# Gated attention's fine levels packed by 32 tokens, eight places for the merge masks of the WKV scan, and two long reciprocals in four column parts

## The chip, the cores and the metric

The kernel runs on one core of a Trainium2 chip. The metric is device time in microseconds, the median of several executions; smaller is better. One further execution was taken with the hardware profiler, and every row below is from that one.

## The reference

Sequence of 512 tokens, width 1024, float32. A first block has two layers (three mixers side by side, then an MLP and a gated embedding), a second block has a banded attention, an RWKV-7 mixer (WKV) and two convolutional FFNs. What the change touches is, cut to its core:

```
# HGRN2 ("gated attention"), 4 heads of 64, in each of the two layers of the first block
G = cumsum(log_f); decay[l, s] = exp(G[l] - G[s]) for s <= l, else 0
A[l, s] = sum_d q[l, d] * decay[l, s, d] * k[s, d]
o = inter + A @ v;  h_out = head_rms_norm(o) * silu(gate)
# mLSTM ("memory"), 4 heads of 64: weighted scores, a denominator, head_rms_norm, a gate
# sliding window attention with a sink, 8 heads, window 128
# WKV, 16 heads of 64, forwards and backwards over the sequence, in the second block:
state = state * w + (state @ a) b^T + v k^T;  y = state @ r
```

## The kernel before

The program is a row of stages with a barrier of all engines between two. Nearly all stages are dense matrix products, which are not changed. Two kinds of stage are.

**The mixers' stage** (`mixers`, once in each of the two layers). Everything lies in SBUF; the tokens are four tiles of 128 (`NT`). Three programs are woven on each engine: attention (16 groups `n` of a head pair and a token tile), gated attention, and memory (8 units, a head pair by a key tile). Each program is a generator that yields a beat before each step, and `weave` emits the steps in the order of their beats; so the constants `MEMORY, UNIT = 0, 4`, `ATTEND, GROUP = 38, 3` and `SCORE, LEVEL = 1, 5.5` set the order on every engine. Engines run their lists in order and wait on semaphores.

Gated attention builds `A` by levels `n` = 0 to 9. Level 0 is the diagonal; level `n` from 1 to 7 has half-width `w = 2^(n-1)` and gives the pairs of a key in the left and a query in the right half of each block of `2w` tokens; levels 8 and 9 are the pairs of different tiles of 128. A level is: VectorE forms two halves of `diffs` (`differ`, L1200 and L1201), ScalarE takes `exp` (L1170), VectorE makes `q_dec` (`decayed`, L1208), TensorE multiplies (`scores`, L1258), and VectorE copies the masked entries from PSUM into `A` (`copy`, L1216). The fine levels 0 to 7 are done for whole 128x128 tiles in two halves `x` (two tiles each), and the second half's products wait until the first half has left PSUM. Levels 8 and 9 are moved by ScalarE (L1181). Then come the sum `A @ v` (L1277), the squares' sums (L1284), a root with an activation table of its own, a reciprocal of 128x512 (L1233), its spread over the heads (L1289) and the gate. Memory ends in the same way: root (L1344), reciprocal (L1379), spread (L1448). Attention's group is: scores (L1063, L1067), peaks (L1118), `exp` on ScalarE, shares (L1135), turn (L1079), take (L1034), outputs (L1094). GpSimd does nothing in this stage.

**The WKV stage** (`rwkv_heads`), a software pipeline over 8 head pairs. Its longest part merges inverses of 64x64 blocks in five levels: 20 units `u` per iteration, in the order of `merge_order`, each with `inner` (L2779) and `outer` (L2792) products on TensorE and two copies on ScalarE. `inner` reads a masked block `NM` that GpSimd makes (`part`, L3057), into one of `PARTS_AHEAD = 4` places. Between the parts GpSimd does other work of the next head pair in `scale_beat` (L3067, L3072, L3076, L3079), at fixed places of the same order; the first two of these (L3067) wait for VectorE.

Of the kernel before, what the change touches and what calls it, by code (L numbers as in the profile page):

```python
# [15 lines left out]
P = 128  # L16
# [49 lines left out]
HG_LEVELS = 7  # L66
# [3 lines left out]
MASKS, MASKS_W = columns(("causal", P), ("levels", HG_LEVELS * P), ("pick", 4 * P), ("groups", P), ("sums", 2 * P), ("back", 2 * P))  # L70
# [5 lines left out]
def constants():  # L76
# [31 lines left out]
    for level in range(HG_LEVELS):  # L108
        w = 1 << level
        same = i // (2 * w) == j // (2 * w)  # L110
        m[:, MASKS["levels"] + level * P:MASKS["levels"] + (level + 1) * P] = same & (i % (2 * w) < w) & (j % (2 * w) >= w)
# [284 lines left out]
SCORE, LEVEL = 1, 5.5  # L396
# [562 lines left out]
def mixers(nc, m, f, dst, table=None):  # L959
# [3 lines left out]
               "g_cleared", "g_diffs", "g_exp", "g_q_ready", "g_scored", "g_copied", "g_moved", "g_summed", "g_taken",  # L963
# [5 lines left out]
    with ExitStack() as tmp, stage(nc, f"mixers{f.layer}", *signals) as (block, s):  # L969
# [179 lines left out]
        A = sb("A", [P, 2, 2, 4, P])  # L1149
# [3 lines left out]
        halves_of = [[(0, 0), (1, 1)], [(2, 2), (3, 3)]]  # L1153
        pieces = [halves_of] * (1 + HG_LEVELS) + [[[(0, 1), (2, 3)]], [[(0, 2), (1, 2)], [(0, 3), (1, 3)]]]
        numbers = [(n, x) for n in range(len(widths)) for x in range(len(pieces[n]))]
        masked = 2 * (1 + HG_LEVELS)

# [8 lines left out]

        def gated_act(act):
# [4 lines left out]
            for n in range(len(widths)):  # L1172
                if n >= 1:
                    yield SCORE + LEVEL * n - 0.5
                    exps(n)
                if n > HG_LEVELS:
                    for x in range(len(pieces[n])):
                        yield SCORE + LEVEL * n + 2.4 + 1.4 * x
                        number = numbers.index((n, x))
                        act.wait_ge(s["g_scored"], number + 1)  # L1180
                        nc.scalar.activation(across[:, number - masked, :, :, :], scores_two(), ACT.Copy).then_inc(s["g_moved"], 1)  # L1181
# [8 lines left out]
        def gated_dve(dve):  # L1190
            yield 0
            nc.vector.memset(A[:], 0.0).then_inc(s["g_cleared"], 1)
            nc.vector.memset(q_dec[:], 0.0).then_inc(s["g_cleared"], 1)

            def differ(n):
                w = widths[n]
                if n >= 3:
                    dve.wait_ge(s["g_scored"], 2 * n - 2)
# [11 lines left out]
            def copy(n, x):  # L1210
                dve.wait_ge(s["g_scored"], 2 * n + x + 1)
                if n == 0:
                    dve.wait_ge(s["g_cleared"], 1)
                at = MASKS["levels"] + (n - 1) * P
                which = (m.masks[:, at:at + P] if n else m.ident).bitcast(I32).unsqueeze(1).unsqueeze(1).broadcast_to([P, 2, 4, P])
                nc.vector.copy_predicated(A[:, x, :, :, :], which, scores_two()).then_inc(s["g_copied"], 1)  # L1216

            for n in range(len(widths)):
# [3 lines left out]
                if n <= HG_LEVELS:  # L1222
                    yield SCORE + LEVEL * n + 2.4
                    copy(n, 0)
                if n + 1 < len(widths):
                    yield SCORE + LEVEL * n + 3
                    differ(n + 1)
                if n <= HG_LEVELS:
                    yield SCORE + LEVEL * n + 3.8
                    copy(n, 1)  # L1230
# [12 lines left out]
        def gated_pe(pe):  # L1243
            def scores(n, x):
                number = numbers.index((n, x))
                if 1 <= number <= masked:
                    pe.wait_ge(s["g_copied"], number)
                elif number:
                    pe.wait_ge(s["g_moved"], number - masked)
                if n >= 1:  # L1250
                    pe.wait_ge(s["g_q_ready"], n)
                kk, qq = (diffs[:, n % 2, :, :], q_dec[:, n % 2, :, :]) if n else (key, hq)
                for i, (source, to) in enumerate(pieces[n][x]):
# [13 lines left out]
            pe.wait_ge(s["g_copied"], masked)  # L1267
            places = {}
            for n, x in numbers:
                for i, pair in enumerate(pieces[n][x]):  # L1270
                    places[pair] = A[:, x, :, 2 * i:2 * i + 2, :] if n <= HG_LEVELS else across[:, numbers.index((n, x)) - masked, :, 2 * i:2 * i + 2, :]
# [15 lines left out]
            pe.wait_ge(s["g_rstd"], 1)  # L1287
# [58 lines left out]
        def memory_dve(dve):  # L1346
# [32 lines left out]
            nc.vector.reciprocal(den[:], den[:]).then_inc(s["c_rstd"], 1)  # L1379
# [9 lines left out]
        def memory_pe(pe):  # L1389
# [56 lines left out]
            pe.wait_ge(s["c_rstd"], 1)  # L1446
            for t in range(2):
                nc.tensor.matmul(m.ps[:, 6 + t, :], const("back", t * P), den[:], start=True, stop=True).then_inc(s["c_back"], 1)  # L1448

# [1061 lines left out]
PARTS_AHEAD = 4  # L2511
# [16 lines left out]
def rwkv_heads(nc, m, a, vec, keep, x_kept):  # L2528


    with ExitStack() as tmp:
# [66 lines left out]
        with stage(nc, "heads", "tables_in", "x_back", f"loaded*8", "set_up",  # L2598
# [445 lines left out]
            def _(pool):  # L3044
# [38 lines left out]
                for i in iterations:  # L3083
# [391 lines left out]
```

## Time and profile before

| what | value |
|---|---|
| median of 3 runs | 3319.1 us (3315.32 to 3321.97) |
| profiled execution, its own time | 3314.73 us |
| its span | 3312.9 us |
| TensorE busy | 3059.1 us, 92% of the span |
| VectorE, ScalarE, GpSimd busy | 1858.7, 1388.3, 630.9 us |
| mean granted clock of TensorE | 0.969 of full speed |

The span is that of the profile; the execution's own time is 1.8 us more than it. The mixers' stages lie at about 164 to 300 us and 924 to 1061 us, the WKV stage at about 2380 to 2870 us.

### The profile page before, as it was taken

How to read it: one execution, taken by the hardware profiler on the slowest of the kernel's cores; microseconds unless marked ns; L12 is line 12 of the kernel's file. 1: busy time of each engine (PE TensorE's matmuls, PEld its weight loads, DVE VectorE, ACT ScalarE, POOL GpSimd, SP SyncE). 2: the span in 40 equal slices, each digit the busy share in tenths (PEclk: the TensorE clock that was granted, in tenths of full speed). 3: DMA queues.
4: the chain of work that ended last, by engine and by line, in shares of the span. 5: the costliest groups of instructions: out<-in, count | busy, mean ns of one | idle time of the engine just before them, and what ended most of it. 6: DMA issues, size and time to landing. Idle time of an engine off the chain costs nothing. (4 is left out here: it accounts for less than half of the span.)

```text
span 3312.9 us, 57356 instructions
## 1 busy us (share of the span) xinstructions
PE 3059.1 (92%) x24238; PEld 2427.1 (73%) x24238; DVE 1858.7 (56%) x2689; ACT 1388.3 (42%) x2363; POOL 630.9 (19%) x528
## 2 busy tenths in 40 slices
PE   8979999999978999999989999979688888799999
PEld 6756788887745788887657888757477777588887
DVE  6675543435675553536575746574366766457464
ACT  5445422235445421234374423345465655344232
POOL 1000220212000220302000101133174554111010
PEclk9989999999989999999899999989899999899999
DMA  4101222222101223232003322225411111033222
GB/s 152 49 1 60 91 95 95 94 95 83 64 4 45 88 94 98 91 101 78 13 9 116 104 91 96 95 105 187 150 35 42 41 39 42 32 101 107 87 97 81
DMA packets 82333, 260.91 MB, mean 79 GB/s; under 512 B 9632, under 2 KB 13216, under 8 KB 81696
## 3 DMA queue, kind: packets, MB, share of 16 engines
q1 hardware_dynamic: 71424, 235.75, 21.9%
q10 hardware_dynamic: 10656, 21.50, 1.7%
q8 instruction: 193, 3.16, 0.4%
q14 instruction: 60, 0.49, 0.0%
HBM read 236.25 MB, written 20.97 MB: 78 GB/s over the span
## 5 line engine op out<-in xcount | busy, mean ns | idle before, releaser
L1654 DVE TENSOR_TENSOR mlp_w_lo<-mlp_ring,mlp_w_hi 128x1024 fp32r<-128x1024 f32 (+1 forms) x211 | 251.6, 1192 | 578.0 <-ACT mlp_w_hi L1631 577.9
L1631 ACT ACTIVATE mlp_w_hi<-mlp_ring 128x1024 fp32r<-128x1024 f32 (+1 forms) x211 | 213.2, 1011 | 647.6 <-PE ps L1592 640.8
L1654 DVE TENSOR_TENSOR ffn_w_lo<-ffn_ring,ffn_w_hi 128x1024 fp32r<-128x1024 f32 (+3 forms) x172 | 224.1, 1303 | 439.2 <-ACT ffn_w_hi L1631 439.2
L1631 ACT ACTIVATE ffn_w_hi<-ffn_ring 128x1024 fp32r<-128x1024 f32 (+3 forms) x172 | 187.2, 1088 | 482.2 <-PE ps L1592 476.7
L1591 PE MATMUL ps<-mlp_more_parts,mlp_w_hi 128*128 128x512 f32 x952 | 373.1, 392 | 0.0
L1590 PE MATMUL ps<-tiles_parts,mlp_w_hi 128*128 128x512 f32 x832 | 329.8, 396 | 1.2 <-issue 1.2
L1590 PE MATMUL ps<-ffn_x_parts,ffn_w_hi 128*128 128x512 f32 x792 | 312.3, 394 | 18.0 <-DVE ffn_x_parts L2369 14.2
L1592 PE MATMUL ps<-tiles_parts,mlp_w_lo 128*128 128x512 f32 x832 | 327.8, 394 | 0.0
L1590 PE MATMUL ps<-mlp_more_parts,mlp_w_hi 128*128 128x512 f32 x760 | 307.0, 404 | 17.5 <-DVE mlp_w_lo L1654 9.1
L1591 PE MATMUL ps<-ffn_x_parts,ffn_w_hi 128*128 128x512 f32 x792 | 309.9, 391 | 0.0
L1592 PE MATMUL ps<-ffn_x_parts,ffn_w_lo 128*128 128x512 f32 x792 | 309.8, 391 | 0.0
L1592 PE MATMUL ps<-mlp_more_parts,mlp_w_lo 128*128 128x512 f32 x760 | 298.2, 392 | 0.0
L1590 PE MATMUL ps<-ffn_hid,ffn_w_hi 128*128 128x512 f32 x632 | 249.8, 395 | 10.9 <-POOL ffn_hid L2203 6.0
L1591 PE MATMUL ps<-tiles_parts,mlp_w_hi 128*128 128x512 f32 x640 | 252.7, 395 | 0.0
L1592 PE MATMUL ps<-ffn_hid,ffn_w_lo 128*128 128x512 f32 x632 | 247.2, 391 | 0.0
L1591 PE MATMUL ps<-ffn_hid,ffn_w_hi 128*128 128x512 f32 x552 | 215.3, 390 | 0.0
L1591 PEld LDWEIGHTS ps<-mlp_more_parts,mlp_w_hi 128*128 128x128 f32 x952 | 180.2, 189 | 40.5 <-issue 3.3
L1717 POOL TENSOR_TENSOR mlp_squares<-mlp_squares,mlp_square 128x512 f32<-128x512 f32 x36 | 52.7, 1464 | 785.7 <-ACT mlp_square L1706 785.5
L1590 PEld LDWEIGHTS ps<-ffn_x_parts,ffn_w_hi 128*128 128x128 f32 x792 | 149.6, 189 | 56.5 <-DVE ffn_x_parts L2369 17.2
L1590 PEld LDWEIGHTS ps<-mlp_more_parts,mlp_w_hi 128*128 128x128 f32 x760 | 144.2, 190 | 56.4 <-issue 13.6
L1590 PEld LDWEIGHTS ps<-tiles_parts,mlp_w_hi 128*128 128x128 f32 x832 | 156.4, 188 | 39.2 <-issue 2.9
L2203 POOL TENSOR_TENSOR ffn_hid<-sq,ffn_hid 128x512 fp32r<-128x512 f32 x44 | 76.4, 1736 | 565.7 <-ACT ffn_hid L2197 565.7
(500 smaller groups left out, 6298.7 us busy)
## 6 DMA issues: line engine op xcount, KB each, us to landing
ffn_ring<-in_w_ffn_up SPq DMA_DIRECT2D x88, 512.0 KB, 3.4
mlp_ring<-in_w_up SPq DMA_DIRECT2D x64, 512.0 KB, 3.4
mlp_ring<-in_w_down SPq DMA_DIRECT2D x64, 512.0 KB, 3.3
rwkv_keep<-ffn_ring ACTq DMA_DIRECT2D x64, 256.0 KB, 2.3
sq<-rwkv_keep SPq DMA_DIRECT2D x64, 256.0 KB, 3.0
ffn_ring<-in_w_ffn_down SPq DMA_DIRECT2D x16, 768.0 KB, 4.4
in_ring<-in_w_in SPq DMA_DIRECT2D x22, 512.0 KB, 3.4
mlp_ring<-in_w_in SPq DMA_DIRECT2D x22, 512.0 KB, 3.4
```

The costliest lines, as they stand in the source:

```text
L1590: nc.tensor.matmul(into, w_hi, hi, start=(part == 0 and k == 0), stop=False, skip_group_check=True)
L1591: nc.tensor.matmul(into, w_hi, lo, start=False, stop=False, skip_group_check=True)
L1592: mm = nc.tensor.matmul(into, w_lo, hi, start=False, stop=ends, skip_group_check=True)
L1631: nc.scalar.activation(w.w_hi[:, n % SPLIT, 0:width], w.ring[:, n % RING, 0:width], ACT.Copy).then_inc(s["w_hi_ready"], 1)
L1654: nc.vector.tensor_tensor(w.w_lo[:, n % SPLIT, 0:width], w.ring[:, n % RING, 0:width], w.w_hi[:, n % SPLIT, 0:width].bitcast(F32), ALU.sub ...
L1717: self.nc.gpsimd.tensor_tensor(w.squares[:], w.squares[:], w.square[:, t % 2, :], ALU.add).then_inc(s[f"{name}_added"], 1)
L2203: nc.gpsimd.tensor_tensor(hidden.lo(p), sq[:, 4 + p % 4, :], hidden.hi(p).bitcast(F32), ALU.subtract).then_inc(s["hid_lo"], 1)
```

## The change

Gated attention: levels 0 to 5 lie within blocks of 32 tokens, so their products are now 32x32 blocks on the diagonal, 64 to a level, in one go; VectorE copies the masked entries from a PSUM area of 2x256 columns into `packed` (128x512), and GpSimd unpacks that once into `A` with four copies. Level 6 is 32 products of 32x32, level 7 is 16 of 64x64; ScalarE places them into `A` without a mask. The two large memsets move from VectorE to GpSimd. `differ(n + 1)` stands ahead of `copy(n)`, and `LEVEL` goes from 5.5 to 4. The two reciprocals of 128x512 are each done in four parts of 128 columns with other work between them. WKV: eight places for `NM`, and the first six parts of an iteration come ahead of GpSimd's other work. The tables of masks shrink.

```diff
-SCORE, LEVEL = 1, 5.5
+SCORE, LEVEL = 1, 4
...
-        A = sb("A", [P, 2, 2, 4, P])
+        A, packed = sb("A", [P, 2, 2 * NT, P]), sb("packed", [P, 2, 2 * NT, HG_W])
...
+        def gated_pool(pool):
+            nc.gpsimd.memset(packed[:], 0.0).then_inc(s["g_cleared"], 1)
+            nc.gpsimd.memset(q_dec[:], 0.0).then_inc(s["g_cleared"], 1)
+            nc.gpsimd.memset(A[:], 0.0).then_inc(s["g_cleared"], 1)
+            pool.wait_ge(s["g_cleared"], 3)
+            pool.wait_ge(s["g_copied"], HG_PACKED)
+            for b in range(P // HG_W):
+                rows = slice(b * HG_W, (b + 1) * HG_W)
+                nc.gpsimd.tensor_copy(A[rows, :, :, rows], packed[rows]).then_inc(s["g_unpacked"], 1)
...
+                if n == HG_PACKED:
+                    yield SCORE + LEVEL * n + 2.4
+                    act.wait_ge(s["g_scored"], n + 1)
+                    act.wait_ge(s["g_cleared"], 3)
+                    for half in range(2):
+                        keys, queries = slice(half * HD, half * HD + HG_W), slice(half * HD + HG_W, (half + 1) * HD)
+                        nc.scalar.activation(A[keys, :, :, queries], scores_of_width(HG_W)[keys], ACT.Copy).then_inc(s["g_placed"], 1)
+                if n == HG_LEVELS:
+                    yield SCORE + LEVEL * n + 2.4
+                    act.wait_ge(s["g_scored"], n + 1)
+                    nc.scalar.activation(A[0:HD, :, :, HD:P], scores_of_width(HD)[0:HD], ACT.Copy).then_inc(s["g_placed"], 1)
...
-            yield 0
-            nc.vector.memset(A[:], 0.0).then_inc(s["g_cleared"], 1)
-            nc.vector.memset(q_dec[:], 0.0).then_inc(s["g_cleared"], 1)
...
-                nc.vector.copy_predicated(A[:, x, :, :, :], which, scores_two()).then_inc(s["g_copied"], 1)
+                nc.vector.copy_predicated(packed[:], which, scores_of_width(HG_W)).then_inc(s["g_copied"], 1)
...
-            nc.vector.reciprocal(g_rows[:], g_rows[:]).then_inc(s["g_rstd"], 1)
+            for part in range(NT):
+                yield SCORE + LEVEL * len(widths) + 9 + 0.75 * part
+                nc.vector.reciprocal(g_rows[:, part * P:(part + 1) * P], g_rows[:, part * P:(part + 1) * P]).then_inc(s["g_rstd"], 1)
...
+                if n <= HG_LEVELS:
+                    if n < HG_PACKED:
+                        w, parts = HG_W, [(e, b * HG_W, b * HG_W) for b, e in ((0, 0), (1, 1), (2, 0), (3, 1), (0, 1), (1, 0), (2, 1), (3, 0))]
+                    elif n == HG_PACKED:
+                        w, parts = HG_W, [(e, half * HD, half * HD + HG_W) for half, e in ((0, 0), (1, 1), (0, 1), (1, 0))]
+                    else:
+                        w, parts = HD, [(0, 0, HD), (1, 0, HD)]
+                    for j in range(NT):
+                        for t in range(2):
+                            for e, of, to in parts:
+                                heads, at = slice(e * HD, (e + 1) * HD), (2 * j + t) * w
+                                mm = nc.tensor.matmul(m.ps[of:of + w, e, at:at + w], kk[heads, t, j * P + of:j * P + of + w],
+                                                      qq[heads, t, j * P + to:j * P + to + w], start=True, stop=True, skip_group_check=True)
+                    mm.then_inc(s["g_scored"], 1)
+                    return
...
-            nc.vector.reciprocal(den[:], den[:]).then_inc(s["c_rstd"], 1)
+            for part in range(NT):
+                yield MEMORY + UNIT * U + 7 + 0.75 * part
+                nc.vector.reciprocal(den[:, part * P:(part + 1) * P], den[:, part * P:(part + 1) * P]).then_inc(s["c_rstd"], 1)
...
-PARTS_AHEAD = 4
+PARTS_AHEAD, PARTS_EARLY = 8, 6
...
-                    for k, t, level, second in merge_order():
-                        if main and not second:
+                    parts = [(t, level) for _, t, level, second in merge_order() if not second]
+                    for t, level in parts[:PARTS_EARLY]:
+                        if main:
                             part(i, t, level)
+                    parts = iter(parts[PARTS_EARLY:])
+                    for k, _, _, second in merge_order():
+                        more = None if second else next(parts, None)
+                        if main and more:
+                            part(i, *more)
                         scale_beat(i + 1, k)
```

What VectorE has for levels 1 and 2 in layer 0 before the change (`mix_weights` is a unit of memory, `mix_diffs` is `differ`):

```order
L1216 COPY_PREDICATED mix_A<-first_masks,ps 128x1024
L1200 TENSOR_TENSOR mix_diffs<-h,tiles 128x256x2
L1201 TENSOR_TENSOR mix_diffs<-h 128x256x2
L1362 SCALAR_TENSOR_TENSOR mix_weights<-ps,mix_weights 128x2x256
L1216 COPY_PREDICATED mix_A<-first_masks,ps 128x1024
L1208 TENSOR_TENSOR mix_q_dec<-tiles,mix_diffs 128x256x2
```

And after it, for the same levels:

```order
L1221 TENSOR_TENSOR mix_diffs<-h,tiles 128x256x2
L1222 TENSOR_TENSOR mix_diffs<-h 128x256x2
L1402 SCALAR_TENSOR_TENSOR mix_weights<-ps,mix_weights 128x2x384
L1237 COPY_PREDICATED mix_packed<-first_masks,ps 128x512
L1229 TENSOR_TENSOR mix_q_dec<-tiles,mix_diffs 128x256x2
```

Two copies of 1024 elements per level have become one of 512, and the next level's `differ` stands ahead of the copy.

GpSimd in an iteration of the WKV stage before, from its first part on (`heads_NM` is a part, the rows on `x` and `sq` are the other work):

```order
L3057 TENSOR_TENSOR heads_NM<-heads_M,heads_masks 128x256 x2
L3067 TENSOR_TENSOR x<-x,sq 128x512
L3057 TENSOR_TENSOR heads_NM<-heads_M,heads_masks 128x256
L3067 TENSOR_TENSOR x<-x,sq 128x512
L3057 TENSOR_TENSOR heads_NM<-heads_M,heads_masks 128x256 x2
L3072 TENSOR_TENSOR x<-x,sq 128x512
```

And after:

```order
L3103 TENSOR_TENSOR heads_NM<-heads_M,heads_masks 128x256 x8
L3113 TENSOR_TENSOR x<-x,sq 128x512
L3103 TENSOR_TENSOR heads_NM<-heads_M,heads_masks 128x256
L3113 TENSOR_TENSOR x<-x,sq 128x512
L3103 TENSOR_TENSOR heads_NM<-heads_M,heads_masks 128x256 x2
L3118 TENSOR_TENSOR x<-x,sq 128x512
```

Eight parts instead of two stand ahead of the first row that waits for VectorE.

## Rows read from the trace of the kernel before

**Rows 1.** The page, part 1: busy time, share of the span, instructions.
```profile
PE 3059.1 (92%) x24238; PEld 2427.1 (73%) x24238; DVE 1858.7 (56%) x2689; ACT 1388.3 (42%) x2363; POOL 630.9 (19%) x528
```

**Rows 2.** Stretches of layer 0's mixers: length, busy time per engine, granted clock, DMA.
```profile
169.00:217.00 48.00, 41.11 (x328) 27.61 (x330) 39.95 (x47) 20.77 (x34) 0.00 (x0) 0.95 0.01 1
217.00:250.00 33.00, 23.12 (x129) 15.91 (x128) 21.46 (x47) 13.50 (x35) 0.00 (x0) 0.69 0.00 0
```

**Rows 3.** The same view for the fine levels' products alone (L1258, PE, PEld).
```profile
169.00:217.00 48.00, 16.73 (x224) 14.53 (x224) 0.95 0.01 1
```

**Rows 4.** VectorE in order of time, one level: start, length, [idle before].
```profile
187.71 1.30 DVE L1216 COPY_PREDICATED mix_A<-first_masks,ps 128x1024 f32<-128x1024 int32 x1 [0.71 <-PE ps L1258]
...
190.28 1.32 DVE L1216 COPY_PREDICATED mix_A<-first_masks,ps 128x1024 f32<-128x1024 int32 x1
191.50 0.67 DVE L1208 TENSOR_TENSOR mix_q_dec<-tiles,mix_diffs 128x512 f32<-128x512 f32 x1
...
193.87 1.30 DVE L1216 COPY_PREDICATED mix_A<-first_masks,ps 128x1024 f32<-128x1024 int32 x1 [0.18 <-PE ps L1258]
```

**Rows 5.** TensorE in order of time, small products (xcount counts records).
```profile
189.07 1.16 PE L1258 MATMUL ps<-mix_q_dec,mix_diffs 64*128 64x128 f32 x16 [0.36 <-DVE mix_A L1216]
190.16 0.50 PE L1403 MATMUL ps<-mix_C_parts,mix_pick 96*128 96x512 f32 x1
...
2428.57 0.63 PE L2779 MATMUL ps<-heads_XT,heads_NM 64*64 64x64 f32 x16
2429.04 0.63 PE L2792 MATMUL ps<-heads_T,heads_X 64*64 64x64 f32 x16
...
2445.17 0.41 PE L2711 MATMUL ps<-heads_BK,heads_A 64*64 64x64 f32 x16
2445.41 0.41 PE L2711 MATMUL ps<-heads_A,heads_BK 64*64 64x64 f32 x16
```

**Rows 6.** TensorE in order of time, start of layer 0's attention.
```profile
223.09 2.08 PE L1258 MATMUL ps<-mix_q_dec,mix_diffs 64*128 64x128 f32 x16 [5.81 <-DVE mix_q_dec L1208]
...
226.98 3.78 PE L1448 MATMUL ps<-mix_den,first_masks 128*128 128x512 f32 x4
...
232.25 0.50 PE L1063 MATMUL ps<-mix_band_parts,mix_ident_parts 128*128 128x256 f32 x2
```

**Rows 7.** VectorE in order of time, memory's reciprocal in layer 0.
```profile
219.06 3.35 DVE L1379 RECIPROCAL mix_den<-mix_den 128x512 f32<-128x512 f32 x1
```

**Rows 8.** TensorE in order of time: sum, attention's last groups, next stage.
```profile
254.81 0.44 PE L1277 MATMUL ps<-mix_A,sq 128*64 128x128 f32 x4
...
259.33 0.71 PE L1079 MATMUL ps<-mix_scaled,mix_p 128*128 128x128 f32 x4
...
284.78 0.80 PE L1063 MATMUL ps<-mix_band_parts,mix_ident_parts 128*128 128x256 f32 x2
...
290.49 0.50 PE L1063 MATMUL ps<-mix_band_parts,mix_ident_parts 128*128 128x256 f32 x2
...
299.84 6.23 PE L1574 MATMUL ps<-c 128*128 128x512 f32 x10 [1.69 <-PEq L148]
```

**Rows 9.** ScalarE in order of time, layer 0's mixers.
```profile
217.73 1.28 ACT L1170 ACT_TABLE_LOAD   x1
219.02 1.06 ACT L1170 ACTIVATE mix_diffs<-mix_diffs 128x1024 f32<-128x1024 f32 x1
...
239.85 1.02 ACT L1181 ACTIVATE mix_across<-ps 128x1024 f32<-128x1024 f32 x1 [3.23 <-PE ps L1258]
```

**Rows 10.** TensorE's waits, 2395 to 2895 us: total, times, longest.
```profile
PE ps L2779 <- POOL heads_NM L3057: 17.9, 15, 1.7
```

**Rows 11.** GpSimd in order of time, first WKV iteration.
```profile
2407.28 2.33 POOL L3057 TENSOR_TENSOR heads_NM<-heads_M,heads_masks 128x256 f32<-128x256 f32 x2
...
2414.41 1.27 POOL L3067 TENSOR_TENSOR x<-x,sq 128x512 f32<-128x512 f32 x1 [2.89 <-DVE x L3198]
```

**Rows 12.** VectorE in order of time, the last input of iteration two's `gram_a`.
```profile
2435.88 0.85 DVE L3227 TENSOR_TENSOR heads_BK<-sq,heads_EN 128x512 f32<-128x512 f32 x1
```

More of the change, by code:

```diff
@@ L69 @@
                            ("rows_in", 4 * 8), ("rows_out", 4 * P))
-MASKS, MASKS_W = columns(("causal", P), ("levels", HG_LEVELS * P), ("pick", 4 * P), ("groups", P), ("sums", 2 * P), ("back", 2 * P))
+MASKS, MASKS_W = columns(("causal", P), ("levels", HG_PACKED * HG_W), ("pick", 4 * P), ("groups", P), ("sums", 2 * P), ("back", 2 * P))
 BANDS1_W = 2 * P
@@ L107, in constants @@
         m[32 * h, MASKS["back"] + at:MASKS["back"] + at + HD] = 1.0
[L108 to L111, printed above, removed]
+    key, query = np.arange(P)[:, None] % HG_W, np.arange(HG_W)[None, :]
+    m[:, MASKS["levels"]:MASKS["levels"] + HG_W] = key == query
+    for n in range(1, HG_PACKED):
+        w, at = 1 << (n - 1), MASKS["levels"] + n * HG_W
+        same = key // (2 * w) == query // (2 * w)
+        m[:, at:at + HG_W] = same & (key % (2 * w) < w) & (query % (2 * w) >= w)
     b1 = np.concatenate([np.where(j > i, 0, NEG), np.where(j <= i, 0, NEG)], 1).astype(np.float32)
@@ L1152, in mixers @@
         widths = [0] + [1 << n for n in range(HG_LEVELS)] + [P, 2 * P]
[L1153 to L1156, printed above, removed]
+        pieces = {HG_LEVELS + 1: [[(0, 1), (2, 3)]], HG_LEVELS + 2: [[(0, 2), (1, 2)], [(0, 3), (1, 3)]]}
+        numbers = [(n, x) for n in range(len(widths)) for x in range(len(pieces.get(n, [0])))]
+        inside = 1 + HG_LEVELS
         def side(ap, w, which):
@@ L1180, in gated_act @@
                         act.wait_ge(s["g_scored"], number + 1)
[L1181 removed]
+                        nc.scalar.activation(across[:, number - inside, :, :, :], scores_two(), ACT.Copy).then_inc(s["g_moved"], 1)
             yield SCORE + LEVEL * len(widths) + 4
@@ L1245, in scores @@
                 number = numbers.index((n, x))
-                if 1 <= number <= masked:
-                    pe.wait_ge(s["g_copied"], number)
+                if 1 <= n <= HG_PACKED:
+                    pe.wait_ge(s["g_copied"], n)
+                elif n == HG_LEVELS:
+                    pe.wait_ge(s["g_placed"], 2)
+                elif number == inside:
+                    pe.wait_ge(s["g_placed"], 3)
                 elif number:
-                    pe.wait_ge(s["g_moved"], number - masked)
+                    pe.wait_ge(s["g_moved"], number - inside)
                 if n >= 1:
@@ L1266, in gated_pe @@
             pe.wait_ge(s["g_moved"], 3)
-            pe.wait_ge(s["g_copied"], masked)
-            places = {}
-            for n, x in numbers:
+            pe.wait_ge(s["g_placed"], 3)
+            pe.wait_ge(s["g_unpacked"], P // HG_W)
+            places = {(j, j): A[:, :, 2 * j:2 * j + 2, :] for j in range(NT)}
+            for n, x in numbers[inside:]:
                 for i, pair in enumerate(pieces[n][x]):
-                    places[pair] = A[:, x, :, 2 * i:2 * i + 2, :] if n <= HG_LEVELS else across[:, numbers.index((n, x)) - masked, :, 2 * i:2 * i + 2, :]
+                    places[pair] = across[:, numbers.index((n, x)) - inside, :, 2 * i:2 * i + 2, :]
             for t in range(2):
```

36 lines of the change are left out of this document (19 added, 17 removed).

## Prediction

> **What bounds the kernel now.** I read the page first. TensorE is busy 92% of the span [rows 1], but that is an average over dense stages, which the change leaves alone. So I looked at the two kinds of stage that it touches, each by busy time in stretches and then engine by engine in order of time.
>
> Fine levels of layer 0's mixers, 169 to 217 us: TensorE is busy 41.1 of 48 us, VectorE 40.0, ScalarE 20.8, GpSimd nothing [rows 2]. TensorE and VectorE pass work to and fro: a level takes 6.16 us from its first masked copy (187.71) to the next level's (193.87), each copy is 1.3 us, and VectorE idles only 0.71 and 0.18 us before one [rows 4]. TensorE waits for the copy too (0.36 us idle, released by the copy) [rows 5]. VectorE is a little the tighter of the two.
>
> Start of attention, 217 to 250 us: TensorE is busy 23 of 33 us at a granted clock of 0.69 [rows 2]. It sat idle for 5.81 us before level 7's products, whose `q_dec` stood on VectorE behind memory's 3.35 us reciprocal [rows 6, 7]. After that the products of 512 columns take 3.78 us for four records [rows 6], at the lower of the two clocks, 1.2 GHz. Attention's third group starts at 232.25 [rows 6], the next stage at 299.84 [rows 8].
>
> WKV stage: TensorE waits 17.9 us in 15 pieces for GpSimd's masked parts [rows 10]. GpSimd has made two parts, then sits 2.89 us idle waiting for VectorE before its other work, with further parts queued behind [rows 11].
>
> **The change, mixers, fine levels.** VectorE's 16 copies of 1.3 us per layer [rows 4] become 6 of half the elements: 20.8 us become about 4, and the memsets go. VectorE then has about 3.2 us per level (a copy of 0.65, three operations of 0.6, a memory unit of 0.75), so the bound moves to TensorE. Its work other than these products is 41.11 - 16.73 = 24.4 us for 8 memory units [rows 2, 3]. The new products are 6 x 64 + 32 + 16 = 432 per layer, two records each, 864 records. What is one worth? No row shows 32x32. The rows show, start to start: 64x128, which can use two parts of the array side by side, 1.09/16 = 68 ns; 64x64 where two parts take turns, 0.47/16 = 29 ns; 64x64 where all four take turns, 0.24/16 = 15 ns [rows 5]. The new order goes round eight parts, so it is nearest to the last; the size gives nothing more if issue is then the limit, and half (7 ns) if it is not. I take 15 ns, so 864 x 0.015 = 13 us in place of 16.7 and the parts of levels 7 that came later. The bounds are 7 and 68.
>
> The Trainium skill speaks against this change here: the page "TensorEngine Tiling (Array Packing)", section Performance Considerations, says that a product costs about 60 cycles however few its columns, and "TensorE: Matmul & The Clock Gate", Part 1, that start to start never drops under about 25 ns. By 25 ns the new products would take 21.6 us per layer, an estimate from that page; the pair of rows at 15 ns in this trace is under it already, so I go by the trace.
>
> TensorE's fine stretch then needs 24.4 + 13 + 1.2 (level 8, as one half of a level now, 1.16 [rows 5]) = 38.6 us from 169. Two hand-overs are not covered: levels 7 and 8 wait until ScalarE, in order, has placed the level before (1.02) and taken the exp (1.06) [rows 9]. That is about 3 us less 1 that memory's products fill: level 8 is through at 209.6. GpSimd's four unpacking copies have some 14 us of cover before the sum needs them. Its memsets (nearest row: 128x512 in 1.27 us [rows 11], so 5 us for 128x2048) end at about 172, before level 1 wants `q_dec` at about 177; without that cover they would cost the difference, up to 2 us.
>
> **Start of attention.** From 209.6 this chain follows: ScalarE's five pieces of memory's tail (3.1, behind the exp of level 8), moving level 8 (1.0), table load and root (1.9), moving the first piece of level 9 (1.0), the second piece's products (1.2), table load and the first group's exps (2.5), its move (1.0), the sum (80 records, 254.81 to 259.33, 4.5 [rows 8]), memory's spread at the higher clock (half of 3.78 = 1.9 [rows 6]); less what runs side by side, about 2. That gives attention's third group at 225.7, against 232.25: 6.5 us earlier, and with levels 7 to 9 and the sum behind it, which before still had to come. VectorE's reciprocal in four parts of about 0.9 us lies inside this chain and holds nothing.
>
> Rest of attention: 13 more starts of a group. Before, the last two took (290.49 - 284.78)/2 = 2.85 us each [rows 8], so 37 us; gated attention's tail on top (two products of 1.9 us, two table loads of 1.28 [rows 9], part of a reciprocal) about 8; from the last group to the next stage 299.84 - 290.49 = 9.35 [rows 8]. Sum 225.7 + 37 + 8 + 9.4 = 280.1, which is 19.7 us before 299.84. TensorE still has short idle stretches in here, and before it dropped to the lower clock in such a place [rows 2]; I set 3 us against that. **Each mixers' stage: -17 us, both -34.** Layer 1 has the same stage, with some table work on VectorE, which has room now.
>
> **WKV.** Eight parts of 0.7 us before the first piece that waits for VectorE. GpSimd then comes to that piece at about 2413.5 instead of 2409.6 and to the second, which waited until 2414.41 [rows 11], about 1 us late. Queued behind it are the inputs of the next iteration; their last one on VectorE ends at 2436.7 and its reader starts at 2445.2 [rows 5, 12], so 8 us of cover, and 1 us is hidden. Where GpSimd is ahead, `inner` and `outer` alternate at 0.47 us [rows 5] without a wait. If all waits went, 17.9 us would go [rows 10]; in later iterations ScalarE's table loads (1.28 [rows 9]) stand in the same stretch and will take over some of it. I take two thirds: **-12 us**; bounds 0 and -18.
>
> 1,200 more records need issuing; as a bound the trace gives no row, I put **+2 us** against gaps in issue.
>
> **Sum:** -34 - 12 + 2 = -44 on the profiled execution's own 3314.7 (span 3312.9 plus 1.8), so 3270.7. The median of the runs, 3319.1, is 4.4 above that execution, so 3275. What a measurement of this kernel can tell from no change is about 0.2%, 6.6 us.
>
> **Rivals.**
> 1. *Small products do not go below the turn-taking pitch.* If 32x32 runs at 29 ns like `inner` [rows 5], 864 x 14 ns = 12 us per layer come back: 3275 + 24 = 3299. For it: weights and product are two instructions per record. Against: 15 ns exists. The skill's 25 ns on the page named above would be this case a little weaker.
> 2. *The waits are gone but their time is not.* WKV's next wait takes all of the 12, or attention stays at the lower clock: 0.69 over 33 us before [rows 2] cost up to 33 x (1 - 0.69) = 10 us per layer, of which I counted most as won. Either gives 3287 to 3293; I say 3290.
> 3. *Better than forecast:* records at 7 ns save 7 us more per layer, or all 17.9 us go in WKV: 3255 to 3262; I say 3257.
> 4. *Slower.* If 32-column pieces cannot overlap and each record costs 68 ns like 64x128 [rows 5], TensorE gets 864 x 53 ns = 46 us more per layer, 92 in all: 3275 + 92 = 3367. This decides from a pitch of 15 + 44/1.728 = 40 ns. For it: new shape, part of the columns only. Against: 64x64 did overlap fourfold.
> 5. *The change does nothing*, both gains hidden by memory's and attention's own chains: 3319.
>
> **Chances.** Forecast 0.47 (own range 3264 to 3284), rival 1 0.17, rival 2 0.14, rival 3 0.12, rival 4 0.06, rival 5 0.04. The range 3250 to 3302 leaves out rivals 4 and 5, 0.10, and the ends of 1 and 3, together under 0.2. Faster by over 0.2%: 0.89; within: 0.04; slower: 0.07, rival 4 and a little of rival 5.
>
> **What the profile after would show.** Fine products in groups of 128 records that start 1.9 us before the next thing on TensorE (3.7 in rival 1, 8.7 in rival 4); levels about 5 us apart (before 6.16); hardly any waits of VectorE's copies on anything but TensorE; level 7 done before attention's first scores; no idle stretch over 2 us on TensorE before the sum; the stage about 119 us long instead of 136; TensorE's waits on `heads_NM` under 3 us. The prediction is wrong if the pitch is over 20 ns, if the granted clock in the fine levels falls clearly under the 0.95 of before [rows 2], or if WKV's iterations keep their length.

## The result, and the profile after

The changed kernel takes 3270.2 us (median of 4 runs, 3260.3 to 3275.9), the kernel before 3317.2 us on the same chip: ratio 0.9857, 95% interval 0.9837 to 0.9876, so 47 us less. Forecast were 3275 and 44 us less. The profiled execution of after is the slowest of its four, 3275.9 us with a span of 3274.1; where this matters (the WKV stage) the other profiles are used. One execution of e6 below took 3904.3 us at a mean granted clock of 0.739 and is left out of its ratio.

The page's first part, after; TensorE has 1,216 records more than in [rows 1] and is busy 13.4 us less:

```profile
PE 3045.7 (93%) x25454; PEld 2419.4 (74%) x25454; DVE 1828.4 (56%) x2677; ACT 1393.8 (43%) x2369; POOL 651.7 (20%) x542
```

Layer 0's mixers by stretches, the same two as in [rows 2] (length, busy time of each engine, granted clock, DMA):

```profile
169.00:217.00 48.00, 40.22 (x1002) 25.55 (x1002) 31.92 (x52) 28.57 (x44) 3.86 (x5) 0.89 0.01 3
217.00:250.00 33.00, 27.58 (x194) 19.16 (x195) 19.66 (x49) 16.90 (x42) 0.00 (x0) 0.80 0.00 0
```

VectorE has 8 us less to do in the first stretch. TensorE does far more in the second, 27.6 us against 23.1, as work has moved into it, at a granted clock of 0.80 in place of 0.69.

TensorE in order of time. L1288 is the packed product (32 columns for levels 0 to 6, 64 for level 7), L1297 those of levels 8 and 9, L1485 memory's sums, L1317 gated attention's sum, L1065 the first scores of a group of attention, L1329 gated attention's spread, L1620 the next stage:

```profile
182.45 1.29 PE L1288 MATMUL ps<-mix_q_dec,mix_diffs 64*32 64x32 f32 x128
...
185.72 1.46 PE L1288 MATMUL ps<-mix_q_dec,mix_diffs 64*32 64x32 f32 x128
187.11 0.50 PE L1445 MATMUL ps<-mix_C_parts,mix_pick 96*128 96x512 f32 x1
...
199.75 0.76 PE L1288 MATMUL ps<-mix_q_dec,mix_diffs 64*32 64x32 f32 x64
...
203.70 1.15 PE L1288 MATMUL ps<-mix_q_dec,mix_diffs 64*64 64x64 f32 x32 [1.15 <-DVE mix_q_dec L1229]
...
207.72 1.16 PE L1297 MATMUL ps<-mix_q_dec,mix_diffs 64*128 64x128 f32 x16 [1.89 <-DVE mix_q_dec L1229]
209.87 3.68 PE L1485 MATMUL ps<-mix_c_squares,first_masks 128*128 128x512 f32 x4 [0.99 <-ACT mix_c_squares L1372]
...
221.26 0.69 PE L1317 MATMUL ps<-mix_A,sq 128*64 128x128 f32 x4
...
228.32 0.80 PE L1065 MATMUL ps<-mix_band_parts,mix_ident_parts 128*128 128x256 f32 x2
...
243.10 3.78 PE L1329 MATMUL ps<-mix_g_rows,first_masks 128*128 128x512 f32 x4 [5.04 <-DVE mix_g_rows L1253]
...
280.34 4.53 PE L1620 MATMUL ps<-c 128*128 128x512 f32 x10 [1.70 <-PEq L150]
...
934.36 0.27 PE L1288 MATMUL ps<-mix_q_dec,mix_diffs 64*32 64x32 f32 x9 [1.22 <-issue]
...
940.55 0.32 PE L1288 MATMUL ps<-mix_q_dec,mix_diffs 64*32 64x32 f32 x22 [1.43 <-issue]
...
1023.72 4.53 PE L1620 MATMUL ps<-c 128*128 128x512 f32 x10 [1.72 <-PEq L150]
```

The idle 5.81 us before level 7 of [rows 6] are now 1.15, level 8 is through at 208.9, and the next stage starts at 280.34, 19.5 us before the 299.84 of [rows 8]. In layer 1 it starts 743.4 us later; before, it was 761.2, so 17.8 more are gained there. The two rows at 934 and 940 us are layer 1's: TensorE stops for 1.22 and 1.43 us inside a row of 128 small products, after 119 and after 106 of them, with nothing that it waits for in the profile ("issue"). Experiment e8 takes this up.

VectorE for one level, to set beside [rows 4] (the levels' copies were 6.16 us apart):

```profile
183.78 0.73 DVE L1237 COPY_PREDICATED mix_packed<-first_masks,ps 128x512 f32<-128x512 int32 x1 [0.82 <-PE ps L1288]
...
187.22 0.73 DVE L1237 COPY_PREDICATED mix_packed<-first_masks,ps 128x512 f32<-128x512 int32 x1 [0.61 <-PE ps L1288]
```

GpSimd: a memset, then, in the first WKV iteration, the eight parts that now stand ahead of the two pieces that wait for VectorE, to set beside [rows 11]:

```profile
165.60 2.08 POOL L1173 MEMSET mix_q_dec<- 128x2048 f32 x1
167.64 1.80 POOL L1174 MEMSET mix_A<- 128x2048 f32 x1
...
2371.42 6.62 POOL L3103 TENSOR_TENSOR heads_NM<-heads_M,heads_masks 128x256 f32<-128x256 f32 x8
2378.00 2.20 POOL L3113 TENSOR_TENSOR x<-x,sq 128x512 f32<-128x512 f32 x1
...
2380.83 1.28 POOL L3113 TENSOR_TENSOR x<-x,sq 128x512 f32<-128x512 f32 x1
```

And TensorE's waits over the stage, where [rows 10] had 17.9 us in 15 pieces:

```profile
PE ps L2825 <- POOL heads_NM L3103: 1.8, 1, 1.8
```

### The profile page after: what moved, and what is told of

It reads as the page before. It is cut to its first block and busy times, and to the rows that moved or that the text cites. A ratio compares the mean times of both kernels' runs of the same rounds, so it can differ in the third digit from the quotient of the medians.

```text
span 3274.1 us, 59784 instructions
## 1 busy us (share of the span) xinstructions
PE 3045.7 (93%) x25454; PEld 2419.4 (74%) x25454; DVE 1828.4 (56%) x2677; ACT 1393.8 (43%) x2369; POOL 651.7 (20%) x542
## 5 line engine op out<-in xcount | busy, mean ns | idle before, releaser
L1638 PEld LDWEIGHTS ps<-tiles_parts,mlp_w_lo 128*128 128x128 f32 x832 | 156.2, 188 | 37.2
## 6 DMA issues: line engine op xcount, KB each, us to landing
ffn_ring<-in_w_ffn_down SPq DMA_DIRECT2D x16, 768.0 KB, 4.2
```

The source lines that it names most:

```text
L1638: mm = nc.tensor.matmul(into, w_lo, hi, start=False, stop=ends, skip_group_check=True)
```

## The experiments

Twelve experiments ran, one of them (e5) the changed kernel once more, each timed against the kernel before on its own chip. The table shows the ratio with its interval and three lengths from each profile: the start of the stage after layer 0's mixers, the distance to the same product of layer 1, and the WKV stage, from its first sum of squares to the next stage's first product.

| kernel | ratio (95%) | layer 0 | to layer 1 | WKV |
|---|---|---|---|---|
| before | 1 | 299.84 | 761.2 | 511.1 |
| after | 0.9857 (0.9837 to 0.9876) | 280.34 | 743.4 | 507.3 |
| e1 WKV part only | 0.9949 (0.9931 to 0.9967) | 297.89 | 764.3 | 495.6 |
| e2 mixers only | 0.9904 (0.9887 to 0.9922) | 277.78 | 743.9 | 511.4 |
| e3 whole reciprocals | 0.9839 (0.9816 to 0.9862) | 275.11 | 738.0 | 497.6 |
| e4 pace only | 0.9969 (0.9957 to 0.9981) | 298.56 | 755.4 | 510.5 |
| e5 after, again | 0.9867 (0.9849 to 0.9885) | 280.43 | 743.9 | 492.4 |
| e6 reciprocals only | 1.0017 (1.0004 to 1.0029) | 296.16 | 765.4 | 523.0 |
| e7 part after part | 0.9945 (0.9931 to 0.9958) | 296.47 | 757.0 | 498.0 |
| e8 products twice | 1.0004 (0.9993 to 1.0015) | 309.34 | 768.0 | 495.1 |
| e9 memory's parts only | 0.9853 (0.9837 to 0.9870) | 275.11 | 737.9 | 502.3 |
| e10 pace of before | 0.9914 (0.9894 to 0.9934) | 286.18 | 751.1 | 503.8 |
| e11 places only | 0.9914 (0.9901 to 0.9927) | 280.66 | 744.0 | 519.1 |
| e12 spread later | 0.9869 (0.9852 to 0.9887) | 279.60 | 745.1 | 498.1 |

**e1 and e2: the two halves.** e1 is the kernel before with `PARTS_AHEAD, PARTS_EARLY = 8, 6` and GpSimd's new order; e2 is the changed kernel with these undone:

```diff
-PARTS_AHEAD, PARTS_EARLY = 8, 6
+PARTS_AHEAD = 4
...
-                    for t, level in parts[:PARTS_EARLY]:
...
+                    for k, t, level, second in merge_order():
+                        if main and not second:
+                            part(i, t, level)
```

Of e1 was expected: 

> The kernel before with only the WKV part of the change (eight places, six parts made early). Theory A, read from the two traces: each of the six repeats between two sums of squares is 1.0 to 2.8 us shorter, 9.9 us in all, and the 6 us that the profiled execution of after lost in the stage's last 75 us belong to a lower granted clock there and not to the change; so 3307 us, 10 less than before (ratio 0.997). Rival B: the waits' time comes back at the end of the stage whatever the clock; then 3314 to 3317 (ratio 0.999 to 1). Rival C: the whole 17.9 us of waits is gained: 3299. The profile should show TensorE's waits for heads_NM under 3 us and the distances of the sums at 46.8 to 59 us as in after.

Of e2: 

> The changed kernel with WKV as before (four places, parts in the old order). Theory A: 3280 us, 37 less than before (two mixers' stages of 19.5 and 17.8 less, as the two traces show; ratio 0.989), and 10 more than after. Rival B, in which WKV gives nothing: 3270 to 3273, as after. The profile should show the stage's next product at about 280.3 and WKV waiting for heads_NM about 18 us again.

WKV alone brings 0.51%, 17 us (11 to 23 by the interval); the mixers alone 0.96%, 32 us (26 to 37). Together that is 49, beside 44 to 47 for the whole, so the halves add. e1 gives more than Theory A's 10 us, near the 17.9 of Rival C. The two profiles of e2's mixers' stages are 39 us shorter than before's, more than its timed runs give. In the profile first e1, then e2 (TensorE's waits over the stage):

```profile
PE ps L2779 <- POOL heads_NM L3057: 2.3, 2, 1.8
```

```profile
PE ps L2825 <- POOL heads_NM L3103: 14.6, 13, 1.7
```

The 507.3 us of WKV in the first profile of after were one execution's; e5, the same kernel once more, has 492.4. At its end, after and e5 (the same kernel) in the same piece of the program, by stretches:

```profile
2790.00:2817.00 27.00, 22.96 (x715) 19.94 (x711) 8.38 (x21) 9.43 (x24) 0.00 (x0) 0.82 0.01 4
```

```profile
2780.00:2805.00 25.00, 20.41 (x734) 18.19 (x730) 8.90 (x22) 10.37 (x27) 0.00 (x0) 1.00 0.01 4
```

The granted clock is 0.82 in the one and 1.00 in the other. The nine profiles with the change in WKV give 492.4 to 507.3, mean 498.9, the five without it or with the places alone 510.5 to 523.0, mean 515.0: 16 us between the means, beside e1's 17.

**e11: places without the order.** The changed kernel with `PARTS_AHEAD = 8` and GpSimd's old order. 

> The changed kernel with GpSimd's order of before in WKV, but eight places. Theory A: GpSimd made only two parts ahead of its first piece that waits for VectorE, and more places don't change that; most of the 18 us of waits on heads_NM stay (over 12) and 12 to 16 us are lost: 3278 to 3284. Rival B: four places were the limit (GpSimd waits for inner to free one): waits under 6 us, 3266 to 3270.

TensorE's waits over the stage, then GpSimd in order of time:

```profile
PE ps L2825 <- POOL heads_NM L3103: 20.3, 17, 1.7
```

```profile
2369.76 2.33 POOL L3103 TENSOR_TENSOR heads_NM<-heads_M,heads_masks 128x256 f32<-128x256 f32 x2
2372.05 1.26 POOL L3113 TENSOR_TENSOR x<-x,sq 128x512 f32<-128x512 f32 x1
2373.28 0.72 POOL L3103 TENSOR_TENSOR heads_NM<-heads_M,heads_masks 128x256 f32<-128x256 f32 x1
2376.90 1.27 POOL L3113 TENSOR_TENSOR x<-x,sq 128x512 f32<-128x512 f32 x1 [2.90 <-DVE x L3244]
```

Theory A: this is the picture of [rows 11] with twice the places, GpSimd sits 2.90 us behind three parts, and the time is that of e2 (0.9914 and 0.9904), a little over A's range. The order is what worked. That it needs the eight places is read from the code (`part` waits for a free place) and was not run: no kernel has the new order with four.

**e4 and e10: the pace.** e4 is the kernel before with `SCORE, LEVEL = 1, 4`, e10 the changed one with `SCORE, LEVEL = 1, 5.5`.

> The kernel before with only the planner's pace between the fine levels changed, 5.5 to 4, which brings each level's instructions earlier in the order of all engines. Theory A: before, VectorE is the bound of a level (6.16 us, two copies of 1.3 us), so levels can't follow each other at 4 and the other work is only pushed behind them: 3310 to 3325 us, within 0.2 per cent of before. Rival B: the pace is what brings most of the gain, because level 9 and the sum stand earlier among attention's groups: 3285 to 3300.

> The changed kernel with the planner's pace between levels as before, 5.5 in place of 4; packing, unpacking and WKV stay changed. Theory A: packing makes room that only the pace uses, since levels are then placed later among memory's and attention's pieces: 15 to 25 us of the mixers' 32 are lost, 3280 to 3292 us. Rival B: every engine takes its work as soon as it can, so the numbers set only the order and little is lost: 3266 to 3274. The pace alone, in the kernel before, gave 0.9969.

The pace alone brings 10 us (0.9969), between the two theories of e4. Without it the change loses 0.5 to 0.6%, 16 to 19 us against the two results of after, as Theory A of e10 has it. So about half of the mixers' 32 us hang on the pace. Of that half the pace brings 10 us in the kernel before too, so what needs packing and pace together is some 6 to 9 us, and that is no more than the intervals leave open. TensorE in e10:

```profile
205.84 1.98 PE L1485 MATMUL ps<-mix_c_squares,first_masks 128*128 128x512 f32 x4 [1.49 <-ACT mix_c_squares L1372]
...
212.52 1.97 PE L1288 MATMUL ps<-mix_q_dec,mix_diffs 64*64 64x64 f32 x32 [4.11 <-DVE mix_q_dec L1229]
```

At the old pace level 7 stands behind memory's sums and what follows them, at 212.5 where after has 203.7, and the stall of [rows 6] is back with 4.11 us.

**e7 and e8: what a 32-column product costs.** e7 turns the loops about:

```diff
-                    for j in range(NT):
-                        for t in range(2):
-                            for e, of, to in parts:
+                    for e, of, to in parts:
+                        for j in range(NT):
+                            for t in range(2):
```

e8 runs `for j in [*range(NT), *range(NT)]`, each product twice into the same place.

> The changed kernel with the loops of the packed products turned about: all eight products of one part of TensorE's array in a row, then the next part, instead of going round the eight parts. Number, shape and results are the same. Theory A, that the measured 9.5 to 11 ns from start to start need the turn-taking: the pitch rises to 29 ns or more as for products in which two parts take turns, 768 x 19 ns = 15 us more of TensorE a layer; as TensorE is the bound of the fine levels 8 to 15 us a layer are seen, 3280 to 3300 us. Rival B, that the pitch is that of the issue whatever the part: 3264 to 3270 as unaltered. Rival C: a part that is loaded again waits for its product, 68 ns as for 64x128: 3340 or more.

> The changed kernel with every product of levels 0 to 7 (those of 32 and of 64 columns) issued twice into the same place, 864 more records a layer: one suspected cost is doubled. Theory A, in which TensorE is the bound of the fine levels and a record costs 10 ns: 8.6 us more of TensorE a layer, of which 6 to 9 are seen, 3277 to 3288 us. Rival B, that VectorE's and ScalarE's chain from level to level bounds them: the products lie in that chain too, but memory's products then fill no gap, and 3 to 5 a layer are seen, 3271 to 3278. Rival C, that the products lie wholly beside other work: 3264 to 3270.

TensorE in e7, then in e8:

```profile
185.15 3.54 PE L1288 MATMUL ps<-mix_q_dec,mix_diffs 64*32 64x32 f32 x128
188.61 0.39 PE L1445 MATMUL ps<-mix_C_parts,mix_pick 96*128 96x256 f32 x1
```

```profile
184.44 1.84 PE L1288 MATMUL ps<-mix_q_dec,mix_diffs 64*32 64x32 f32 x187
188.66 0.95 PE L1288 MATMUL ps<-mix_q_dec,mix_diffs 64*32 64x32 f32 x69 [2.38 <-issue]
...
194.54 1.76 PE L1288 MATMUL ps<-mix_q_dec,mix_diffs 64*32 64x32 f32 x174
198.49 1.09 PE L1288 MATMUL ps<-mix_q_dec,mix_diffs 64*32 64x32 f32 x82 [2.18 <-issue]
...
212.10 1.46 PE L1288 MATMUL ps<-mix_q_dec,mix_diffs 64*32 64x32 f32 x149
214.82 1.11 PE L1288 MATMUL ps<-mix_q_dec,mix_diffs 64*32 64x32 f32 x107 [1.27 <-issue]
...
225.44 1.45 PE L1468 MATMUL ps<-mix_weights,h 128*96 128x384 f32 x4 [1.25 <-issue]
...
228.99 0.25 PE L1288 MATMUL ps<-mix_q_dec,mix_diffs 64*32 64x32 f32 x4 [0.92 <-issue]
```

e7: 3.46 us for 128, 27 ns from start to start, and levels 5.5 to 6.9 us apart. The time rises by 0.8 to 0.9%, 26 to 29 us, the upper end of Theory A. The same products that go round the eight parts take 9.5 to 11 ns (after: 1.22 to 1.43 us for 128), so the turn-taking is worth 16 us in layer 0 alone (296.47 against 280.43).

e8 fits none of its theories: 45 to 49 us more, and 28.9 us in layer 0, 33 ns for each of 864 added products whose pitch in the rows is 10. In every row of doubled products of levels 0 to 6 TensorE stands still once with nothing that it waits for in the profile ("issue"). The gap opens after 199, 187, 174, 162, 149, 136 and 124 products of the row, so it is no fixed length of row that opens it. Counted from gap to gap over all of TensorE's products, the distance is 255 or 256 five times in a row and then 128 twice, where one gap (225.44) lies on a unit of memory and not on small products. The changed kernel has gaps at the same distances: in layer 1 they lie 127 products apart, and in e5's layer 0 the two are 382 apart, three times that. So the gaps sit at fixed places of TensorE's program, about 128 products with their weight loads apart, and e8, which has twice the small products between the longer ones, shows more and longer gaps (0.9 to 2.4 us). e7, where the same products take 27 ns, shows none in layer 0.

In layer 0 seven of e8's gaps lie on small products, 11.6 us in all (TensorE's waits, 169 to 300 us), an eighth of 1.3 us on memory's, and the granted clock of the fine levels is 0.66, against 0.86 in e5 and 0.90 in after (the stretch from 169 to 212 us):

```profile
PE ps L1288 <- issue: 11.6, 7, 2.4
```

```profile
169.00:212.00 43.00, 33.77 (x1080) 21.17 (x1080) 15.87 (x25) 9.66 (x16) 0.69 (x1) 0.66 0.01 3
```

e5 has 1.8 us of gaps there, so 11 us of the 28.9 are added gaps, at most 8.6 the products themselves (864 at 10 ns), and the rest goes with the lower clock. That clock follows the gaps: in stretches of 5 us e8 has 0.50 at 179, 189 and 199 us, each behind a gap of about 2 us, where e5 has 0.94 to 1.00 (memory's `weights` products there take 2.87 us for four of 384 columns, in e5 1.53). The places of the gaps are measured; that they come from the supply of TensorE's instructions is argued from their even distance and from "issue", and no run changed the supply.

**e3, e6, e9: the reciprocals in parts.** e3 has both whole in the changed kernel, e6 is the kernel before with both in parts, e9 the changed one with gated attention's whole:

```diff
-            for part in range(NT):
-                yield SCORE + LEVEL * len(widths) + 9 + 0.75 * part
-                nc.vector.reciprocal(g_rows[:, part * P:(part + 1) * P], g_rows[:, part * P:(part + 1) * P]).then_inc(s["g_rstd"], 1)
+            nc.vector.reciprocal(g_rows[:], g_rows[:]).then_inc(s["g_rstd"], 1)
```

> The changed kernel with both long reciprocals of 512 columns in one piece again. Theory A: in after, VectorE has room where memory's reciprocal stands, but the piece of 3.35 us is put ahead of q_dec and the copies of one level; the first one costs up to 3 us a layer, the second (gated attention's) up to 1: 3274 to 3278 us (4 to 8 more than after). Rival B: TensorE's chain at the start of attention hangs on ScalarE's order and not on VectorE: 3269 to 3272, no difference from after. Rival C: most of the mixers' gain was this stall of 5.8 us a layer: 3280 or more.

> The kernel before with only the two long reciprocals in four parts. Theory A, that the stall of 5.81 us on TensorE before level 7 came from memory's reciprocal ahead of q_dec: about 3 us a layer less, 3308 to 3311 us, and the stall at 223 us down to about 3. Rival B, that the chain hangs on ScalarE and on the fine levels' pace: no difference, 3313 to 3318. Rival C, from the experiment with whole reciprocals in the changed kernel, where each mixers' stage was 5 us shorter than with four parts: the parts cost, 3322 to 3327.

> The changed kernel with gated attention's reciprocal whole again and memory's still in four parts. Theory A, from the profiles of the changed kernel and of the one with both whole: gated attention's four parts let attention's small operations in between, so TensorE waits 5.04 us instead of 3.36 for g_rows, and its clock is 0.66 in the 10 us around it instead of 0.92; memory's parts do neither good nor harm. Then this kernel is as fast as the one with both whole: ratio 0.984 (3255 to 3262 beside a before of 3311), with a wait of about 3.4 us and one reciprocal of 3.35 us. Rival B: memory's parts are the costly ones: 0.9865. Rival C: the parts make no difference at all and the two results differ by chance: 0.985 to 0.987 and the wait is still 5 us.

VectorE and then TensorE in e5 (four parts); the same two in e3 (whole):

```profile
237.85 1.76 DVE L1253 RECIPROCAL mix_g_rows<-mix_g_rows 128x128 f32<-128x128 f32 x2 [3.15 <-ACT mix_g_rows L1213]
...
241.12 1.76 DVE L1253 RECIPROCAL mix_g_rows<-mix_g_rows 128x128 f32<-128x128 f32 x2
```

```profile
242.94 3.78 PE L1329 MATMUL ps<-mix_g_rows,first_masks 128*128 128x512 f32 x4 [5.04 <-DVE mix_g_rows L1253]
```

```profile
235.02 3.35 DVE L1251 RECIPROCAL mix_g_rows<-mix_g_rows 128x512 f32<-128x512 f32 x1 [3.15 <-ACT mix_g_rows L1213]
```

```profile
238.43 3.59 PE L1327 MATMUL ps<-mix_g_rows,first_masks 128*128 128x512 f32 x4 [3.36 <-DVE mix_g_rows L1251]
```

Between the second and the third part VectorE does 1.5 us of attention's small operations, and TensorE has nothing else to do until all four are there: 5.04 us of waiting where e3 has 3.36 (in layer 1 5.6 where e3 has 3.4). The stretch around it, which e3 reaches 4.5 us earlier, has its clock at 0.57 in e5 and 0.76 in e3 (over 10 us, set against each other in the same way, 0.66 and 0.83):

```profile
240.00:247.00 7.00, 4.06 (x7) 2.00 (x8) 5.42 (x17) 1.08 (x5) 0.00 (x0) 0.57 0.00 0
```

```profile
235.50:242.50 7.00, 4.07 (x10) 2.16 (x11) 6.65 (x17) 2.36 (x6) 0.00 (x0) 0.76 0.00 0
```

So all three expectations for e3 missed: it is not slower, and in the profile faster. In e6 it is the same, 4.6 us instead of 2.7, while the stall before level 7 only goes from 5.8 to 4.8: in the kernel before, ScalarE's exp for that level ends only at 220.1, 2.8 us into the stall, behind memory's root and two table loads, so at most 2.3 us of the stall are the reciprocal's (to 222.41). e6 is 0.17% slower than before, some 6 us, half of its Rival C; its profiled execution is the slowest of the eleven behind the ratio and has 523.0 us in WKV, where nothing is changed. e9, with memory's in parts and gated attention's whole, has the lengths of e3 (275.1 and 737.9), so memory's parts do nothing and what the parts cost lies with gated attention's.

The 5.2 and 5.5 us by which e3 and e9 are under the first profile of after are not all of that cost. The last product before this reciprocal is gated attention's sum of squares; TensorE in e5, then in e3:

```profile
231.04 1.98 PE L1324 MATMUL ps<-tiles,first_masks 128*128 128x512 f32 x4
```

```profile
228.20 1.98 PE L1322 MATMUL ps<-tiles,first_masks 128*128 128x512 f32 x4
```

e3 is 2.8 us ahead there already, before the parts can matter, and so is e2 (228.40), which has the parts. From here to the next stage the four profiles with parts (after, e5, e2, e11) take 49.1 to 49.4 us in layer 0 and 50.2 to 50.4 in layer 1, e3 and e9 46.9 and 47.5. The parts of gated attention's reciprocal cost 2.5 us in layer 0 and 2.7 in layer 1, in every profile; where the rest comes from is open. In the timed runs 5 us are smaller than the table's intervals: 0.9839 and 0.9853 without these parts, 0.9857 and 0.9867 with them. The sign fits, but a gain of the whole kernel from taking them out isn't settled.

**e12: the spread one group later.** With both reciprocals whole, the two products that wait for `g_rows`, the scaling and the gating get later numbers:

```diff
-            yield SCORE + LEVEL * len(widths) + 12
-            pe.wait_ge(s["g_rstd"], 1)
+            yield SCORE + LEVEL * len(widths) + 15
+            pe.wait_ge(s["g_rstd"], 1)
```

> The changed kernel with both reciprocals whole and gated attention's spread (the two products that wait for g_rows), scaling and gating one group later in the order of TensorE and VectorE. Theory A: the wait of 3.36 us for g_rows (5.04 with parts) goes, since a group's products lie in its place, and the clock stays up behind it: 3 to 5 us a layer less than with both whole, ratio 0.981 to 0.983 (3248 to 3256 beside 3311). Rival B: VectorE's chain of the groups is the bound there and takes the time back: 0.984. Rival C: the scaling now stands in the last groups' way: 0.985 or more.

TensorE in e12, then VectorE:

```profile
241.89 2.08 PE L1081 MATMUL ps<-mix_scaled,mix_p 128*128 128x128 f32 x8 [4.96 <-DVE mix_scaled L1137]
```

```profile
236.89 3.35 DVE L1251 RECIPROCAL mix_g_rows<-mix_g_rows 128x512 f32<-128x512 f32 x1 [3.15 <-ACT mix_g_rows L1213]
```

The wait for `g_rows` is gone and one of 4.96 us for `scaled` stands in its place: VectorE itself sits 3.15 us waiting for the root, does the reciprocal, and only then the next group's small operations, for which TensorE now waits. From the sum of squares to the next stage e12 takes 49.5 us in layer 0 and 51.7 in layer 1, 2.6 and 4.2 us more than e3, and nothing is gained (Rival C's size, 0.9869). The reciprocal would have to move as well, behind a group's operations; that wasn't tried.

## Why the prediction was right, and where its steps were off

- **The bound of a fine level.** The mechanism holds. VectorE's copies fell to 0.73 us and TensorE became the engine that sets the levels, 3.3 to 5.1 us apart. In 169 to 217 us VectorE is 16 us idle, TensorE 8. One of the prediction's own signs of being wrong did show: the granted clock of this stretch is 0.89 (0.85 in e5), under the 0.95 of [rows 2]. It is not the small products that lower it. From 179 to 209 us it is 1.00 (e5: 0.99); the lower level stands at the start of the stage, to about 175 us (e5: 179, before: 174), and behind level 8, 0.66 at 209 to 214. In e5 the longer start puts level 8 2.7 us later than in after.
- **The pitch.** I took 15 ns, by the nearest row; it is 9.5 to 11 ns (11.6 in the first row, at the lower clock), so a layer's products take under 10 us and not 13. Rival 1 (29 ns) is refuted for this order, and e7 shows that it was no phantom: in another order of the same products it is 27 ns and costs 26 to 29 us, a little over the 24 that I gave it. By the Trainium skill, page "TensorE: Matmul & The Clock Gate", Part 1, starts are never under about 25 ns apart; the trace disagrees where parts take turns (9.5 to 11 ns) and agrees where they don't (27).
- **Issue gaps, +2.** Mis-sized. After has 1.0 us of them in layer 0's fine levels and 3.7 in layer 1's, on products and behind them, about 5 us (e5: 1.8 and 4.3); the faster pitch pays for it. e8 shows that this term was the dangerous one, since gaps grow when more small products lie between the fixed places of the program. None of my rivals had it.
- **Level 8 and attention's third group.** Level 8 is through at 208.9 (209.6 predicted). The third group comes at 228.3 instead of 225.7, since memory's sums (3.68 us for what takes 1.98 at the higher clock) and the first part of the gated sum (0.69 for 0.44) ran at the lower clock. The rest up to the next stage took 52.0 us, where I had 54.4, and so the stage's end is right (280.34, by the sum 280.1) through two errors of 2.5 us with opposite signs, which is luck. The 3 us a layer that the forecast set against idle stretches made 17 of these 19.7; they were not needed in layer 0. Both mixers' stages: 37 us by the profiles, 32 (26 to 37) by e2's runs, predicted 34.
- **"VectorE's reciprocal in four parts of about 0.9 us lies inside this chain and holds nothing."** This is said of memory's, and it holds (e3 and e9 have equal stages). Gated attention's stands only as "part of a reciprocal" in the 8 us of the tail, and there the four parts cost: TensorE waits 1.7 to 2.2 us a layer more, and the stage is 2.5 to 2.7 us longer (e3, e9). The prediction asked what a shorter piece lets in and not who waits for the last piece. It also read the whole 5.81 us before level 7 as memory's reciprocal; e6, with both in parts in the kernel before, takes 1 us off.
- **The pace.** The prediction treated it as part of the packing. e4 and e10 show it to be worth 10 us (6 to 14) without the packing and 16 to 19 with it.
- **WKV, -12.** The right mechanism, a term probably too small: 17 us in e1, though its interval (11 to 23) still holds the 12; the profiles' means differ by 16. I left a third of the 17.9 us to ScalarE's table loads and other waits; by these figures most of it was gained, as rival 3 had it in its second half. GpSimd's second waiting piece comes 2.3 us later behind the parts' start than before, not 1 us, and the 8 us of cover took that too: GpSimd still idles 9.98 us before the next iteration's first piece. e11 confirms that GpSimd's order and not its places was at fault.
- **GpSimd's memsets.** 2.08 and 1.80 us in place of the estimated 5, over by 169.4, no cost.
- **Rival 2** (waits gone, time not) had its chance in the first profile of after, whose WKV stage was only 4 us shorter; the other eight profiles and e1's time refute it. Rivals 4 and 5 are refuted by the result. Rival 3 (better than forecast) had both its conditions half right, a faster pitch (10 ns, not 7) and nearly all of WKV's waits, and yet the kernel is at 3270 and not 3257; the gaps in issue and gated attention's parts, 5 us each, stand against it. The forecast of 44 us less for measured 47 thus rests on the right mechanisms and on terms whose errors cancel in part.

## What to carry to other kernels

When an in-order engine serves two others, look first at what is queued in front of the work that is waited for: here six pieces made early, with the buffers to hold them, brought 17 us and the four more buffers alone none. Before cutting a long operation into parts, ask whether its reader needs the first part or the last; if it needs all of them, what slips in between delays the reader. And small products are cheap only as long as neighbours use different parts of the array, and many of them in little time can bring gaps that no semaphore explains: look for "issue" in the waits and count the products from gap to gap.

## What the runs showed of the hardware

- Products of 64 rows by 32 columns that go round eight parts of the array start 9.5 to 11 ns apart (128 in 1.2 to 1.4 us); several in a row on one part 27 ns apart (e7). At a granted clock of 0.50 the same took 11.6 ns (after, 128 in 1.48 us from 173.05) and 44 ns (e7, 128 in 5.65 us from 173.62): the lower clock costs much in the second order and little in the first.
- TensorE stood 0.9 to 2.4 us at places of its program 127 or 128 products apart, or a multiple of that (e8: 255 or 256 five times, then 128 twice; after, layer 1: 127; e5, layer 0: 382). Not every such place has a gap. The granted clock was 0.50 over 5 us that begin within 2 us behind gaps of 1.9 to 2.4 us (e8).
- GpSimd's memset of 128x2048 numbers of four bytes took 1.80 to 2.08 us, less than two of its additions and subtractions of 128x512 (1.27 us each).
- The same kernel's WKV stage was 507.3 us in one execution and 492.4 in another, at a lower and a higher granted clock near its end; a single profile doesn't resolve a change of 10 us there.
